# A transformer block with 32 experts on one core: a first gather 128 columns wide, and w_down of experts 12 and 22 in nine transfers

## What is computed

```python
h = h + hybrid_mixer(rms_norm(h, norm_mix_g[l]), ...)
hn = rms_norm(h, norm_ffn_g[l]).reshape(b * s, d)
h = h + moe_ffn(hn, w_router[l], b_router[l], w_gate_up[l], b_gate_up[l], w_down[l], b_down[l]).reshape(b, s, d)
```

## Time and profile before

| what | value |
|---|---|
| median of 3 runs | 1127.24 us (1127.17 to 1127.55) |
| the profiled execution | 1131.17 us |
| its span, first to last instruction | 1129.4 us |
| TensorE busy with matmuls | 1089.1 us, 96% |
| VectorE, ScalarE busy | 293.7 us, 136.3 us |
| mean granted clock of TensorE | 0.985 |
| moved by DMA | 436.72 MB, 387 GB/s over the span |

### The profile page before, as it was taken

How to read it: one execution, slowest core, us unless ns; L and a number is a source line. 1 busy time by engine, 2 the same in 40 slices (tenths; PEclk the granted TensorE clock), 3 DMA queues, 4 the chain that set the end, 5 groups by cost and what they waited for, 6 DMA issues and landing times.

```text
span 1129.4 us, 11872 instructions
## 1 busy us (share of the span) xinstructions
PE 1089.1 (96%) x5275; PEld 481.4 (43%) x5275; DVE 293.7 (26%) x677; ACT 136.3 (12%) x232; POOL 8.3 (1%) x16
## 2 busy tenths in 40 slices
PE   9999999999999999999999968999999999999997
PEld 5678897533333333333333324333333333333332
DVE  2788742331111111121111110212111111111111
ACT  1425340110000000000000000100000000000001
POOL 0100000000000000000000000000000000000000
PEclk9999999999999999999999987999999999999999
DMA  8533488699999999999999999999999999999996
GB/s 313 231 150 138 161 319 357 263 400 402 430 428 438 439 430 425 435 435 428 435 430 424 436 420 426 430 429 436 427 433 430 433 432 430 431 424 428 427 424 261
DMA packets 21652, 436.72 MB, mean 387 GB/s; under 512 B 2496, under 2 KB 2880, under 8 KB 6272
## 3 DMA queue, kind: packets, MB, share of 16 engines
q1 hardware_dynamic: 21072, 435.27, 91.1%
q10 hardware_dynamic: 528, 0.68, 0.2%
HBM read 434.89 MB, written 1.05 MB: 386 GB/s over the span
## 4 chain that ended last, share of the span: by engine, by line
PE 79%; DMA 17%; DVE 3%; issue 1%; SPq 1%; ACT 0%; ACTq 0%; DVEq 0%
PE Pp L1019 33%; PE Bp L1033 14%; DMA gate_up_room<-in_w_gate_up 12%; PE Pp L701 4%; PE Ap L1047 4%; DMA odd_down<-in_w_down 3%; PE Bp L1005 3%; PE Pp L650 3%; PE Pp L666 2%; PE Pp L901 2%; PE Ap L912 2%; PE Bp L1026 1%; PE Pp L690 1%; DVE odd_down L1630 1%; DMA odd_down<-in_b_down 1%; PE Pp L961 1%
## 5 line engine op out<-in xcount | busy, mean ns | idle before, releaser
L1019 PE MATMUL Pp<-gate_up_room,OBT 128*64 128x512 f32 x2048 | 453.4, 601 | 13.8 <-DMA gate_up_room<-in_w_gate_up 13.8
L1019 PEld LDWEIGHTS Pp<-gate_up_room,OBT 128*64 128x64 f32 x2048 | 147.0, 139 | 303.7 <-issue 279.9
L1619 DVE TENSOR_SCALAR odd_down<-Pp 128x512 f32<-128x512 f32 x31 | 21.4, 692 | 618.2 <-PE Pp L1019 618.2
L1033 PE MATMUL Bp<-even_down,odd_down 128*64 128x512 f32 x512 | 113.7, 595 | 1.2
L1033 PE MATMUL Bp<-odd_down 128*64 128x512 f32 x480 | 106.3, 595 | 1.8 <-DVE odd_down L1630 0.6
L1820 ACT ACTIVATE odd_down<-odd_down 128x512 f32<-128x512 f32 x30 | 18.9, 630 | 476.0 <-DVE odd_down L1619 476.0
L1047 PE MATMUL Ap<-odd_down,cst 64*128 64x512 f32 x256 | 65.4, 630 | 5.2 <-DMA odd_down<-in_b_down 4.5
L1033 PEld LDWEIGHTS Bp<-even_down,odd_down 128*64 128x64 f32 x512 | 35.2, 137 | 69.1 <-issue 63.3
L1033 PEld LDWEIGHTS Bp<-odd_down 128*64 128x64 f32 x480 | 33.1, 137 | 65.3 <-issue 59.9
L1005 PE MATMUL Bp<-X,cst 128*64 128x512 f32 x240 | 56.6, 592 | 0.0
L701 PE MATMUL Pp<-odd_down,gate_up_room 128*128 128x128 f32 x448 | 53.2, 277 | 0.5 <-DVE odd_down L1370 0.5
(11 more groups left out here) (227 smaller groups left out, 698.3 us busy)
## 6 DMA issues: line engine op xcount, KB each, us to landing
gate_up_room<-in_w_gate_up SPq DMA_DIRECT2D x14, 4096.0 KB, 23.6
gate_up_room<-in_w_gate_up SPq DMA_DIRECT2D x27, 2048.0 KB, 42.7
even_down<-in_w_down SPq DMA_DIRECT2D x11, 4096.0 KB, 36.0
odd_down<-in_w_down SPq DMA_DIRECT2D x11, 4096.0 KB, 39.6
gate_up_room<-in_w_in SPq DMA_DIRECT2D x8, 2048.0 KB, 7.4
even_down<-in_w_down SPq DMA_DIRECT2D x7, 2048.0 KB, 17.5
odd_down<-in_w_down SPq DMA_DIRECT2D x6, 2048.0 KB, 21.1
odd_down<-in_w_down SPq DMA_DIRECT2D x7, 1024.0 KB, 21.6
```

Source lines behind the costliest of these rows:

```text
L1019: last = mm((Gps, Ups)[q // 2][64 * (q % 2):64 * (q % 2) + 64, :], xT[:, k % 4, k // 4, :], quarter(e, w, q), start=False, stop=k == KC - ...
L1033: last = mm(bank[64 * hf:64 * hf + 64, :], turned[:, c, s, :], w[:, c * 1024 + hf * 512:][:, 0:512], start=s == 0 and c == 0, stop=s == DN ...
L1619: V.tensor_scalar(gm, Gps, LIMIT, None, ALU.min).then_inc(d_gm, 1)
```

## The change

The first gather's moving operand becomes 128 columns: the 64 of `OH` and 64 columns of zeros beside them, on the left for token block 0 and on the right for block 1. The zeros are written by two memsets on VectorE, behind the last gate sum, into parts of `GT`'s and `PG`'s places that aren't in use yet. Each product so writes 64 more columns of PSUM and adds zeros there; the results move by 64 columns in `Tps` and lie from 192 on in `Yps`. TensorE waits for the memsets (`v_zero`) once, before the first of the four calls.

W_down of experts 12 and 22 is issued as nine transfers in place of one: seven of 16 partitions each (r, r+8, r+16, ... for r = 0 to 6) and two of 8 partitions (7, 23, 39, ... and 15, 31, 47, ...). Rows, bytes and places are the same. `signals` returns 9 for them, and TensorE waits for all nine.

```diff
+UNEVEN = (12, 22)
...
+        one_hot_beside_zeros = [ofl[:, 192:320], ofl[:, 320:448]]
...
+            if i == GU and e in UNEVEN:
+                return 9
...
-            return (Tps[:, 0:256], Yps[:, 256:512])[r].rearrange("p (c s) -> p c s", c=4)
+            return (Tps[:, 64:320], Yps[:, 192:448])[r].rearrange("p (c s) -> p c s", c=4)
...
                 if e in EIGHT:
                     released(e, TURNS - 1)
+                    if e in UNEVEN:
+                        for first, step in [(r, 8) for r in range(7)] + [(7, 16), (15, 16)]:
+                            sp.dma_start(downs[e % 2][first:P:step, :], dn_rows(e)[first:P:step, :])\
+                                .then_inc(full(e, GU), 16)
+                        return
                     sp.dma_start(downs[e % 2], dn_rows(e)).then_inc(full(e, GU), 16)
...
             def gather_first(b, r):
 
+                bank, at = ((Tps, 64 * b), (Yps, 128 + 64 * b))[r]
                 for k in range(4 * r, 4 * r + 4):
-                    last = mm(first_tokens(r)[:, k % 4, :], first_features(X[:, b, :], k), OH[:, b, :],
+                    c = at + 64 * (k % 4)
+                    last = mm(bank[:, c:c + P], first_features(X[:, b, :], k), one_hot_beside_zeros[b],
                               start=b == 0 and k == 0, stop=b == 1, skip_group_check=True)
...
+            pe.wait_ge(v_zero, 2)
             pe.wait_ge(d_oh, 1)
             gather_first(0, 0)
...
             gate_last(7)
+            dve.wait_ge(v_gate, 7)
+            V.memset(ofl[:, 192:256], 0.0).then_inc(v_zero, 1)
+            V.memset(ofl[:, 384:448], 0.0).then_inc(v_zero, 1)
```

More of the change, by code:

```diff
@@ L275, in hybrid_block @@
         m_half, a_half = sem("m_half"), sem("a_half")
-        v_xs = sem("v_xs")
+        v_xs, v_zero = sem("v_xs"), sem("v_zero")
         v_ws = [sem(f"v_ws{u}") for u in range(6, 10)]
```

## The result

The changed kernel takes 1164.75 us (median of 6 runs, 1162.58 to 1171.7), the kernel before beside it 1127.78 us: ratio 1.032, 95% interval 1.030 to 1.034. It is 37 us slower where 3.7 us faster was forecast. The profiled execution is the longest of the six, 1171.7 us with a span of 1169.6.

The account below looks back on a forecast made before the run. The weights' stream at 432 GB/s was taken to bound the kernel (29.1 us an expert, TensorE 26.4). Terms -1.5 - 2.2 = -3.7 us from the 1127.24 median gave 1123.5 us; 8-in-10 range 1122.5 to 1146.

Parts of the forecast that it names:

- part 2: W_down of experts 12 and 22 in nine transfers: relieves eight late DMA engines of one row per expert, -2.2 us.
- the term of -2.2 us: At the weight stream's end: 2 x 1.21 = 2.4 us off the late engines, less 0.1 per transfer for semaphores.
- Part 1, clock and holes: Wider first gather keeps TensorE's clock up; expert 0's products 1.66 us shorter, two holes in the weight stream close.
- The term of -1.5 us: Closing two early stream holes, 1.6 us of standstill, through earlier buffer releases by expert 0; bounds 0 and 1.7 us.
- the rule against it: For the w_down transfers: earlier 32-partition transfers moved at 205 GB/s against 415, 2.02 times slower; the new ones reach 16 partitions.
- the earlier trace: b_down's two 32-partition loads beside the stream: 6.0 us for 0.13 MB, where half rate would be 9.7, full 4.9.
- The first rival: Port halving: w_down rows of experts 12 and 22 take 2.45 us, 1145.3 us if late engines have seven; chance 0.32.
- its worse form: Rows at half rate in w_down of experts 12 and 22, with late engines moving nine: +24.8 - 1.5, 1150.5 us.
- Which half is late: At the stream's end, late engines were taken to get seven rows; rival that they get nine: 1128.3 us, chance 0.11.
- The step at one half: DMA share near 0.5 at the stream's end, two engine halves 5.2 us apart; forecast to shrink to 0.4 and vanish.
- The instruction fetches: Likely cause of the late half: 16 KB fetches of about 1.2 us, four on each of eight engines, 5 us.
- Semaphores and issues: The nine w_down transfers: semaphore writes cost 0.1 us a transfer; SyncE's issues, 3 or 38 us for nine, taken as 0.

Follow-up runs that it names:

- eight equal transfers: Against the change: w_down of experts 12 and 22 as eight strided transfers of 16 partitions (r, r+8, ...), wider gather kept; 1159.09 us, ratio 1.026.
- smaller clashes: Against the wider gather alone: w_down of experts 12 and 22 as 7/8 of columns in one transfer, the rest in 16 transfers of 8 partitions; 1135.06 us.

## Why the prediction was wrong

The step that failed is in part 2: that a 32 KB row takes 1.21 us also in a transfer to 16 strided partitions. It was measured at 2.49 to 2.51 us, and the term of -2.2 us became a loss of 37.2.

**Part 1, clock and holes: right where it acts.** The clock stayed up, the products fell from 15.40 to 13.91 us, the holes closed. The memsets, the wait and the wider products cost nothing that a run can tell. What failed in this part is a silent step, that the one execution profiled stands for all. The term of -1.5 us applies to the executions in which the clock falls; in the others there is nothing to close. What is left is 1.1 to 1.3 us in the mean; in the median it is 0.4 us in one series and 2.1 in the other, since half of the runs of the kernel before, more or less, are long ones.

**Part 2, the rule against it: the wrong row was taken as the nearer.** The prediction had both rows, with 205 for 415 GB/s and the earlier trace rows with 6.0 us for 0.13 MB, and chose the second since it lay in the same stage. It should have been the first: the earlier trace rows are 64 rows of 2 KB (and 32 semaphore writes) beside a stream, whose own time says little about two large rows that meet for their whole length. Nor did the prediction look at the neighbours: in the same 12 us the stream's 64 KB rows took 2.64 us on average, 3.22 at most, where 2.42 is usual; how much of that is a clash of places and how much the sharing of an engine by two queues, the trace doesn't tell. The runs bear the clash out: 2.49 to 2.51 us a row strided by eight, 3.56 in blocks, 1.22 strided by four, full rate by columns. The Trainium skill ("SBUF — State Buffer", section on the DMA port swizzle) gives the partitions' ports, and its order holds here: sixteen ports reached, full rate (1.22 us a row); eight, half (2.49); four, worse still (3.56). By its ports alone, as an estimate, the blocks would take 4.8 us a row. The issue order of the same transfers, which leaves the ports reached by each as they are, changes a row from 2.49 to 2.15 us.

**The first rival: right in kind, too small.** It had a chance of 0.32. Its row of 2.45 us was within 3%. It gave 1145.3 us, or 1150.5 in its worse form; measured are 1164.75. Three terms were missing. Engines in normal rows pay too when strided ones meet them at the borders: up to 6.44 us for a row of 2.42, so that each expert of eight equal transfers costs 15.8 us rather than the 10 of its own rows. The unequal shares end in one or two engines that run behind alone, 5.7 us. And the second expert costs more than the first, 15.6, then 21.6, as the engine that ends last loses more than the average one. The range's upper end, 1146, left the worse form out at the cost of the case that came.

**Which half is late: most likely right, and of no use.** The step at one half disappears with unequal shares and stays with equal ones, so the early engines most likely did get the nine rows. That was a guess, and the prediction called it one. But the step "A row less in two experts relieves the late eight by 2 x 1.21 = 2.4 us" did not hold either where it was tried with smaller clashes: 7.5 us were lost where 2.4 were to be gained. The likely reason, that the row's place still has to take it, is argued and not isolated. Why the halves are 5 us apart wasn't tested. The instruction fetches last 1.06 us each rather than 1.2; 34 of them behind 229 us would be 4.5 us for each of eight engines (an estimate).

**Semaphores and issues:** 0.1 us a transfer agrees with at most 0.09 measured; issues stayed hidden, even 28.6 us for nine of them.

None of the kernels run is clearly faster than the kernel before. The best is the wider gather alone, 0.9992 and 0.9993 in two series, both intervals to 1.0003 (these ratios are not the quotients of the medians above, which lie closer to 1 in the first series and further off in the second).

## What to carry to other kernels

In a saturated stream look at where each engine writes, not only at how much: a transfer that puts two engines at one place costs the difference in full (1.3 us a row here), and its neighbours pay as well. In neither way tried here did handing rows from late engines to early ones gain anything. To cut a load into pieces, cut it by columns, over all 128 partitions, or take every fourth partition; both ran here at the full rate, while every eighth partition and blocks of 16 did not. Where the runs of a kernel lie in two groups, profile it more than once before a term of the sum rests on one execution.

## What was not expected of the hardware

- The granted clock behind the same gather fell to half in three executions of the kernel before and stayed at 1.00 in a fourth, with TensorE busy all of the 3.5 us in each; once the products were 128 columns wide it was at 1.00 in every one of thirteen profiles.
- Nine transfers of 128 partitions with runs of 3.6 KB took SyncE 28.6 us to issue at expert 12, most of it in the last three, and at expert 22 one of nine took 18.9 us; those of 16 partitions with runs of 32 KB took 0.54 to 0.66 us each.
- Order matters: the same eight transfers in the order 0, 4, 1, 5, ... moved a row in 2.15 us instead of 2.49.
- In the change one engine lay 7.4 us behind the next one at the landings of 944.7, 993.2 and 1105.4 us, and still 5.9 us at 1154.6: as long as the stream was full it did not catch up. With eight equal transfers it was 0.5 us (landing at 982.7 us).
